# Delta heads through tanh inside local attention's steps, and the first projection block loaded in halves

## The reference

```python
def ab_mixer(u, w_in, conv_w, a_log, dt_bias, a_out_g, bq_g, bk_g, sink, w_out):
    proj = u @ w_in
    qa, ka, va, za, ba, aa, qb, kb, vb = split_cols(proj, AB_SIZES)
    ya = delta_mixer(qa, ka, va, za, ba, aa, conv_w, a_log, dt_bias, a_out_g)
    ...
    yb = window_mixer(qb, kb, vb, sink)
    return jnp.concatenate([ya, yb.astype(ya.dtype)], axis=-1) @ w_out

def delta_mixer(hq, hk, hv, hz, hb, ha, conv_w, a_log, dt_bias, o_gain):
    qkv = jax.nn.silu(centred_conv(jnp.concatenate([hq, hk, hv], axis=-1), conv_w))
    q, k, v = split_cols(qkv, (A_QKW, A_QKW, A_VW))
    q = l2norm(q.reshape(bsz, n, A_HEADS, A_DK)) * (A_DK ** -0.5)
    k = l2norm(k.reshape(bsz, n, A_HEADS, A_DK))
    ...
```

## Time and profile before

| | us |
|---|---|
| three runs | 1564.33, 1565.94, 1567.14; median 1565.94 |
| the profiled execution | 1562.62 |
| its span | 1560.8 |
| busy: PE, PEld | 1520.3 (97%), 1471.7 (94%) |
| busy: DVE, ACT, POOL | 1099.1 (70%), 798.1 (51%), 173.7 (11%) |
| local attention's steps and the tail behind them | 54 to 142 |
| the delta stage | 142 to about 245 |

### The profile page before, as it was taken

How to read it: one execution, slowest core, us unless ns; L and a number is a source line. 1 busy time by engine, 2 the same in 40 slices (tenths; PEclk the granted TensorE clock), 3 DMA queues, 4 the chain that set the end, 5 groups by cost and what they waited for, 6 DMA issues and landing times.

```text
span 1560.8 us, 31984 instructions
## 1 busy us (share of the span) xinstructions
PE 1520.3 (97%) x12908; PEld 1471.7 (94%) x12908; DVE 1099.1 (70%) x1965; ACT 798.1 (51%) x1369; POOL 173.7 (11%) x187
## 2 busy tenths in 40 slices
PE   6988999999999999999999999999999999999997
PEld 5977899999998999999998999999999999999997
DVE  5784758676778677778778667776668666666666
ACT  4766445343455544446545655444555556554443
POOL 2481203000021200002000201000010010200000
PEclk9998999999999999999999999999999999999999
DMA  6420016454441345454433424656444444356561
GB/s 223 163 109 1 3 55 213 174 184 180 162 162 68 109 169 208 162 202 176 163 137 134 166 101 141 216 165 209 168 162 163 162 164 161 109 176 202 166 210 58
DMA packets 124791, 236.35 MB, mean 151 GB/s; under 512 B 2614, under 2 KB 50025, under 8 KB 124665
## 3 DMA queue, kind: packets, MB, share of 16 engines
q1 hardware_dynamic: 123177, 230.24, 42.2%
q0 software_dynamic: 1296, 4.28, 0.9%
q10 hardware_dynamic: 192, 0.05, 0.0%
HBM read 233.51 MB, written 1.05 MB: 150 GB/s over the span
## 4 chain that ended last, share of the span: by engine, by line
PE 88%; DVE 6%; ACT 2%; issue 2%; POOL 1%; DMA 0%; ACTq 0%; DVEq 0%; POOLq 0%
PE ps L675 49%; PE ps L722 6%; PE ps L721 6%; PE ps L720 6%; PE ps L683 6%; PE ps L844 2%; DVE w_lo L2511 2%; PE ps L821 1%; PE ps L771 1%; PE ps L806 1%; DVE hidden L2562 1%; PE ps L831 1%; POOL square_sum L3567 0%; DVE chain_memory L3124 0%; ACT w_hi L1771 0%
## 5 line engine op out<-in xcount | busy, mean ns | idle before, releaser
L1771 ACT ACTIVATE w_hi<-raw 128x1024 fp32r<-128x1024 f32 x440 | 460.6, 1051 | 282.1 <-PE ps L722 135.3
L2511 DVE TENSOR_TENSOR w_lo<-raw,w_hi 128x1024 fp32r<-128x1024 f32 x440 | 547.0, 1243 | 9.4 <-ACT w_hi L1771 9.1
L675 PE MATMUL ps<-u_hi,w_hi 128*128 128x256 f32 (+1 forms) x1464 | 422.6, 289 | 1.9 <-issue 1.2
L675 PE MATMUL ps<-u_hi,w_lo 128*128 128x256 f32 (+1 forms) x1464 | 416.8, 285 | 0.0
L675 PE MATMUL ps<-u_lo,w_hi 128*128 128x256 f32 (+1 forms) x1464 | 416.3, 284 | 0.0
L675 PEld LDWEIGHTS ps<-u_hi,w_hi 128*128 128x128 f32 x1464 | 278.0, 190 | 8.0 <-issue 5.6
L675 PEld LDWEIGHTS ps<-u_hi,w_lo 128*128 128x128 f32 x1464 | 278.1, 190 | 0.0
L675 PEld LDWEIGHTS ps<-u_lo,w_hi 128*128 128x128 f32 x1464 | 277.0, 189 | 0.6
L675 PE MATMUL ps<-a_hi,w_hi 128*128 128x256 f32 x800 | 226.7, 283 | 0.6 <-DVE hidden L2562 0.3
L675 PE MATMUL ps<-a_lo,w_hi 128*128 128x256 f32 x800 | 224.9, 281 | 0.0
L675 PE MATMUL ps<-a_hi,w_lo 128*128 128x256 f32 x800 | 224.8, 281 | 0.0
(11 more groups left out here) (469 smaller groups left out, 2257.1 us busy)
## 6 DMA issues: line engine op xcount, KB each, us to landing
raw<-in_w_ff_dram SPq DMA_DIRECT2D x32, 2048.0 KB, 7.7
raw<-in_ffn_w_gu_dram SPq DMA_DIRECT2D x44, 1024.0 KB, 6.9
raw<-in_ffn_w_down_dram SPq DMA_DIRECT2D x10, 2048.0 KB, 8.0
raw<-in_xa_w_kv_dram SPq DMA_DIRECT2D x8, 2048.0 KB, 8.3
raw<-in_od_w_in_dram SPq DMA_DIRECT2D x6, 2048.0 KB, 7.8
raw<-in_w_in_ab_dram SPq DMA_DIRECT2D x5, 2048.0 KB, 7.9
raw<-in_ev_w_in_dram SPq DMA_DIRECT2D x5, 2048.0 KB, 7.8
raw<-in_xa_w_q_dram SPq DMA_DIRECT2D x4, 2048.0 KB, 7.6
```

The costliest lines, as they stand in the source:

```text
L675: mm = pe.matmul(bank[:, 0:n], wx[:, q, k * P:(k + 1) * P], x[ux][:, k, ts], start=k == 0 and i == 0, stop=k == KD - 1 and i == 2)
L1771: act.activation(quarter(w_hi, b, q), raw_quarter(b, q), ACT.Copy).then_inc(high_split, 1)
L2511: dve.tensor_tensor(quarter(w_lo, b, q), raw_quarter(b, q), quarter(w_hi, b, q).bitcast(F32), ALU.subtract)\
```

## The change

1. The SiLU over all heads becomes x (1 + tanh(x / 2)), twice the SiLU, in three parts of four heads. ScalarE makes the tanh (`half_tanh`) and VectorE the product (`double_silu`): queries in step 3, keys with the tanh in step 5 and the product in step 6, values with the tanh at the end of step 6 and the product in step 8. The factor two is taken out in the squares, in `delta_norm` and in the values' copies. A table set that has both tanh and exponential is loaded in step 2; the set with the logarithm behind the values' tanh.
2. The squares go to steps 4 (queries) and 6 (keys); both are waited for before the key sum.
3. Chunk 11 is convolved as the others are, its products on ScalarE in step 6, its additions on GpSimd.
4. From step 5 on the order changes on three engines: the scores of units 7 and 8 and the key sum come earlier on TensorE; the exponentials of units 7 and 8 come directly behind the copies of pair 6 on ScalarE; on VectorE pair 7's logits come ahead of two tile reads.
5. GpSimd's identity tiles wait for the query sum too.
6. Block 2 is loaded as two halves of 256 columns. The first is issued when two quarters of block 0 are split, and ScalarE waits for it alone before the first two quarters.

```diff
@@ weights, SyncE and ScalarE
-    add("ab_qkvz", [[cols(x, c)] for c in range(0, 2048, BLOCK)])
+    add("ab_qkvz", [[cols(x, 0, 256), cols(x, 256, 256, into=256)]] + [[cols(x, c)] for c in range(BLOCK, 2048, BLOCK)])
...
+                if b == phases["ab_qkvz"].first:
+                    for half, (into, width, source) in enumerate(loads):
+                        sp.wait_ge(low_split, 4 * (b - 2) + 2 * half + 2)
+                        sp.dma_start(raw[:, b % 2, :, into:into + width], source)\
+                            .then_inc(raw_in[b % 2] if half else first_half_in, 16)
+                    return
@@ TensorE
-                pe.wait_ge(M["d_sq"], which + 1)
+                pe.wait_ge(M["d_sq"], 2)
...
+                    pe.wait_ge(M["silu_done"], SILU_TURN[VALUE_HEADS])
@@ ScalarE
+            def half_tanh(which):
+                act.wait_ge(M["conv_done"], 4 * SILU_TURN[which])
+                act.activation(delta_tanh[which], delta_heads[which], ACT.Tanh, scale=0.5).then_inc(M["delta_tanh"], 1)
+            def head_squares(which):
+                act.wait_ge(M["silu_done"], SILU_TURN[which])
+                act.activation(delta_sq[which], delta_heads[which], ACT.Square, scale=0.5).then_inc(M["d_sq"], 1)
...
-                    act.wait_ge(M["conv_done"], 8 if c == 10 else c - 3)
+                    act.wait_ge(M["conv_done"], {10: 8, 11: 10}.get(c, c - 3))
...
+                if k == 5:
+                    half_tanh(KEYS)
+                if k == 6:
+                    conv_products(11)
                 if k < WINDOW_UNITS:
                     window_copies(k)
                 if k == 6:
-                    act.wait_ge(M["conv_done"], 11)
-                    act.wait_ge(M["conv_last"], 1)
-                    act.activation(qkv, qkv, ACT.Silu).then_inc(M["silu_done"], 1)
+                    window_exponents(7)
+                    head_squares(KEYS)
+                    window_exponents(8)
+                    half_tanh(VALUE_HEADS)
                     log_and_exp()
@@ VectorE
+            def double_silu(which):
+                dve.wait_ge(M["delta_tanh"], SILU_TURN[which])
+                dve.scalar_tensor_tensor(delta_heads[which], delta_tanh[which], 1.0, delta_heads[which], ALU.add, ALU.mult)\
+                    .then_inc(M["silu_done"], 1)
...
-                if k == 5:
-                    last_conv()
@@ GpSimd
-            for c in range(11):
+            for c in range(12):
...
-            pool.wait_ge(M["conv_done"], 11)
+            pool.wait_ge(M["conv_done"], 12)
+            pool.wait_ge(M["d_qsum"], 2)
```

More of the change, by code:

```diff
@@ L395, in program @@
             for i, loads in enumerate(ph.blocks):
-                so_far[len(landed_at) % 2] += 16 * len(loads)
+                halved = len(landed_at) == phases["ab_qkvz"].first
+                so_far[len(landed_at) % 2] += 16 if halved else 16 * len(loads)
                 landed_at.append(so_far[len(landed_at) % 2])
@@ L1464, in _ @@
             for k in range(WINDOW_UNITS + 1):
-                if k < WINDOW_UNITS and k != 7:
+                if k < 7:
                     window_scores(k)
-                if k < 7:
                     qkvz_tile(2 * k + 2)
+                if k == 6:
+                    window_scores(7)
                 if k == 0:
@@ L1484, in _ @@
                 if k == 6:
[L1485 removed]
+                    window_scores(8)
                     qkvz_tile(15)
+                if k == 7:
+                    delta_sum(KEYS)
                 if k == 8:
@@ L1766, in split_high @@
                     return
-                if q == 0:
+                halved = b == phases["ab_qkvz"].first
+                if halved and q == 0:
+                    act.wait_ge(first_half_in, 16)
+                if q == (2 if halved else 0):
                     act.wait_ge(raw_in[b % 2], looped(landed_at[b], LOOP_LANDED, g))
@@ L2128, in _ @@
                     next_split(1)
-                if k < 6:
+                if k < 5:
                     conv_products(2 * k)
-                if k < WINDOW_UNITS:
+                if k < 7:
                     window_exponents(k)
+                if k == 5:
+                    conv_products(10)
+                if k == 2:
+                    nc.scalar.preload_act_table_set("exp_and_others")
+                if k == 3:
+                    half_tanh(QUERIES)
+                if k == 4:
+                    head_squares(QUERIES)
                 if k < 6:
@@ L2146, in _ @@
                     conv_products(2 * k + 1)
-                if k == 7:
-                    act.wait_ge(M["silu_done"], 1)
-                    for which in (KEYS, QUERIES):
-                        act.activation(delta_sq[which], delta_heads[which], ACT.Square).then_inc(M["d_sq"], 1)
+                if k == 5:
+                    half_tanh(KEYS)
+                if k == 6:
+                    conv_products(11)
                 if k < WINDOW_UNITS:
@@ L2163, in _ @@
                 act.activation((v_tok if source == 8 else k_tok)[0:n, m], tile_bank[i % 4][0:n, 0:4 * P].rearrange(
-                    "p (h d) -> p h d", h=4), ACT.Copy).then_inc(M["d_copied"], 1)
+                    "p (h d) -> p h d", h=4), ACT.Copy, scale=0.5 if source == 8 else 1.0).then_inc(M["d_copied"], 1)
             def decays(chain):
@@ L2846, in _ @@
             ab = phases["ab_qkvz"].first
-            def last_conv():
-                link(dve.tensor_scalar(qkv[:, 11], xa[:, 11, 0:T], col("conv", 11), None, ALU.mult))
-                for j in range(1, 5):
-                    ins = dve.scalar_tensor_tensor(qkv[:, 11], xa[:, 11, j:j + T], col("conv", 12 * j + 11), qkv[:, 11],
-                                                   ALU.mult, ALU.add)
-                    if j < 4:
-                        link(ins)
-                ins.then_inc(M["conv_last"], 1)
             def project_qb(i, t, gt):
@@ L2962, in delta_norm @@
                 dve.wait_ge(M["d_rs"], which + 1)
-                dve.scalar_tensor_tensor(heads, heads, P ** -0.5 if which == QUERIES else 1.0,
+                dve.scalar_tensor_tensor(heads, heads, 0.5 * P ** -0.5 if which == QUERIES else 0.5,
                                          delta_r[which].rearrange("p h t -> p (h t)"), ALU.mult, ALU.mult)\
                     .then_inc(M["d_normed"], 1)
+            def double_silu(which):
+                dve.wait_ge(M["delta_tanh"], SILU_TURN[which])
+                dve.scalar_tensor_tensor(delta_heads[which], delta_tanh[which], 1.0, delta_heads[which], ALU.add, ALU.mult)\
+                    .then_inc(M["silu_done"], 1)
             dve.wait_ge(M["sink_meta"], 1)
             for k in range(WINDOW_UNITS + 1):
-                if k < WINDOW_UNITS:
+                if k < 7:
                     window_logits(k)
-                if k < 8:
+                if k < 6:
                     qkvz_step(2 * k + 1)
+                if k == 6:
+                    double_silu(KEYS)
+                if k == 7:
+                    window_logits(8)
                 if k < WINDOW_UNITS:
                     window_normalise(k)
+                if k == 6:
+                    window_logits(7)
+                    qkvz_step(13)
+                if k == 7:
+                    qkvz_step(15)
+                if k == 8:
+                    double_silu(VALUE_HEADS)
                 if k == 1:
```

22 lines of the change are left out of this document (12 added, 10 removed).

## The result

The changed kernel takes 1555.83 us (median of 5 runs, 1555.29 to 1560.35), the kernel before, run beside it, 1566.09 (5 runs, 1564.33 to 1567.14). The ratio is 0.9947, with a 95% interval of 0.9936 to 0.9959: 10.3 us faster. The forecast was 1557.5, in a range of 1552.5 to 1562. In a second session five more runs of the changed kernel had a median of 1556.57, against 1564.43 for before (0.9951, 0.9939 to 0.9964).

A forecast was written before the change was run, and what follows sets the result against it. TensorE was taken as the bound, except in the local-attention tail, where waits on VectorE and ScalarE leave holes. The delta stage 8.4 us earlier takes the median from 1565.94 to 1557.5; 8-in-10 range 1552.5 to 1562.

The forecast's parts named there:

- Pairs 2 to 5 cost nothing: Local attention up to pair 5: added ScalarE and VectorE work fits in 8.65 us pairs, TensorE stays the bound; no change.
- Pair 6: Pair 6's transposes start at 110.4, not 115.28: 4.9 us won, nearly all from the convolution removed from VectorE.
- The queue that carries the tail: GpSimd's additions end at 119.0, then values' tanh to 120.1, table load to 121.4, copies 7 to 122.3, key logarithms to 123.9.
- The sums: Key and query sums on TensorE: 2.1 us each at full clock, plus half a microsecond for one at low clock.
- Together: The whole tail: delta stage starts at 134.0 instead of 142.43, 8.4 us earlier.
- The load in halves, 0 with a possible guard of up to 3.3: Block 2's load near 40 us: only ScalarE's idle time goes, counted 0; slack 0.3 us, at most 3.3 against later landings.
- The rest of the span as long as before (1418.4): Sign of being right: everything from the delta stage's start to the end keeps its length, 1418.4 us.
- The slower rival, GpSimd late: Tail additions averaging 1.55 us make GpSimd 12.7 late: 4.3 slower, 1570.2; chance 0.04.
- The convolution's going: Removing VectorE's 3.7 us convolution beside GpSimd was to pay back up to 2.6 us lost to two double SiLUs.

The follow-up runs named there:

- conv_off: The kernel before with chunk 11's convolution moved from VectorE to ScalarE and GpSimd, SiLU and block 2's load still whole; 1565.06 us, ratio 1.0005.
- halves_only: The kernel before with block 2 loaded in halves and nothing else; 1564.78 us, ratio 1.0006.
- before_again: The kernel before, unchanged, run again for a second profile; 1565.13 us, ratio 0.9996.
- pool_longer: The changed kernel with three of chunk 11's products made by GpSimd instead of ScalarE; 1559.33 us, ratio 0.9967 to before.
- whole_load: The changed kernel with block 2 loaded whole again, everything else kept; 1562.70 us, ratio 0.9985 to before.
- whole_again: The changed kernel with block 2 loaded whole, a second time; 1561.65 us, ratio 0.9971 to before.
- whole_late_small: The changed kernel with block 2 loaded whole and GpSimd's four small loads issued only after it has landed; 1562.22 us, ratio 0.9977 to before.
- combined: The changed kernel, halves kept, GpSimd's small loads behind block 2's landing, result 6 and copies 7 ahead of the values' tanh; 1559.54 us, ratio 0.9963 to before.
- early_copies: The changed kernel with pair 6's result and pair 7's copies on ScalarE ahead of the values' tanh and table load; 1556.33 us, ratio 0.9953 to before.
- spin: The changed kernel with five unused 272-column matmuls on TensorE behind the key sum; 1557.90 us, ratio 0.9954 to before.

## Why the prediction was right, point by point

- *Pairs 2 to 5 cost nothing:* right. VectorE was put at 8.5 and measured 8.58, ScalarE at 7.8 and 7.71, TensorE busy throughout. Pair 6's scores start 70.6 us behind the head sum in both kernels.
- *Pair 6:* transposes predicted at 110.4, found at 110.89; pair 7's at 118.7 and 118.01; the key sum at 119.4 and 118.61. The working gave nearly all of pair 6's gain to the removed convolution. At pair 6 that holds (3.4 us by conv_off), but not at the end: conv_off's time is that of before.
- *The queue that carries the tail:* the right queue, and a little short. Convolution 9 was to end at 110.6, and ended at 112.1. The additions took 1.02 each, less than the 1.06 assumed, but their unbroken run now begins at 106.06 and not at 104.20. The addition beside the queries' double SiLU is 0.9 longer than the median, which accounts for half of that delay, and the one beside the keys' adds 1.1 within the run. So the values' tanh started 1.35 after the predicted end of GpSimd at 119.0, and the logarithms at 123.58 instead of 122.3. That the table load costs 1.28 and no drain held: the tanh ends at 121.46, the load at 122.75, and the next activation starts at 122.77. The Trainium skill ("ScalarE: Activation LUTs", What ACT_TABLE_LOAD costs) would add 1.38 there; this trace does not agree.
- *The sums:* half a microsecond was put in for a low clock. In this execution the query sum alone took 3.83 for 2.1, as the window at 0.50 shows. To offset it, the turned tiles ran at full clock, 2.79 instead of 4.46: from the first turn to the delta stage 3.7, where 5.2, measured at a granted clock of 0.66, was assumed. And a term was missing: pair 7's values and unit 8's transposes (2.4 us from 123.72) stand on TensorE between pair 7's copies and the query sum, which began at 126.10, 0.95 behind the end of the logarithms.
- *Together:* the delta stage 8.4 earlier was predicted. It was 6.6 in the first profile (135.84 against 142.43) and 8.1 in the second (134.35). In the first profile the errors are 1.3 (logarithms), 0.95 (the missing term) and 1.2 (clock) the one way and 1.5 (turned tiles) the other, 1.8 in all. That they cancel in part is luck.
- *The load in halves, 0 with a possible guard of up to 3.3:* the step that was mis-sized. Against the kernel before it is 0 (halves_only), but only as that kernel's block is in time. Loaded whole in the changed kernel the block lands 3 us later, and without the halves 5 to 7 us of the 10 would have been lost: 2.5 to 2.7 of wait and 1.7 of low clock on the path, the rest not located. The time was met only because the change carried the halves. The working saw the 0.3 us of slack and named the halves a guard. It did not ask what would make the block later in the new kernel, and its chances had no rival for it.
- *"The rest of the span as long as before (1418.4)":* wrong as a check. 1418.4 was a lucky rest: before_again had 1422.0, the changed kernel 1422.7 and 1420.7. The difference of medians was 10.3 in the first session and 7.9 in the second, that of leads 6.7 and 8.0. In the first the changed kernel's profile was of its slowest run, so the two need not agree. The forecast, made from the median of before, stayed right.
- *The slower rival, GpSimd late:* did not happen, and its place was the right one: at 1.02 per addition ScalarE waits 2.89 us there, and pool_longer shows that a further delay goes straight into ScalarE's wait. In the working's own sum GpSimd sets the tail even without being late; the 8.4 us of this rival are what would use up the whole gain. The Trainium skill ("SBUF — State Buffer", Who interferes with whom) has a VectorE instruction with two inputs in SBUF and a GpSimd instruction that reads SBUF take turns, which the prediction took as up to 2.6 us for the two double SiLUs. The trace agrees in kind: the additions beside them took 1.70 and 1.85 instead of 0.78, 2.0 us in all. In the 14 profiles every addition or product of a convolution on GpSimd that took over 1 us, 198 of them, lay beside a double SiLU or a split (`split_low`, 1.2 to 1.7 us, two inputs in SBUF as well). The mean of 1.02 against 1.06 hides this, as both runs have such neighbours. The convolution's going did not pay it back, as the working had it: the four additions beside it before took 0.90 each, 0.5 us too much in all.

```profile
106.71 3.61 POOL L3595 TENSOR_TENSOR mx<-mx 128x272 f32<-128x272 f32 x4
```

No run moves the double SiLUs away from GpSimd's additions, so what the tail would gain by it is not measured.

## What to carry to other kernels

When an engine's queue has one long operation over data of several producers, splitting it so that only the last part stands behind the last producer is worth more than moving the producer: here the split and its order gave nearly all the gain, the moved convolution 1 to 2 us by the medians, within their intervals. When a queue of small instructions on GpSimd bounds a stage, look at its longest ones and at what VectorE does beside them; a mean over the queue hides them. Where a transfer is in time by a few tenths of a microsecond, guard it in the same change, since another edit may delay it, as happened here, and count a hole in TensorE with the low clock behind it. Before comparing parts of two profiles, look at the granted clock of the parts that were not changed: two profiles of one kernel differed by 3.6 us there.

## What the runs showed of the hardware

- A hole of 2.0 to 2.7 us in TensorE in a stretch that was otherwise busy was followed by a granted clock of 0.66 to 0.93 in the next windows, which cost another 1.7 us (whole_load, whole_again, whole_late_small, combined). Not every such hole is: in early_copies the query sum behind one of 2.51 us ran at full clock (2.10).
- GpSimd's additions over 128x272 took 0.78 us in the median. All 198 additions and products of the convolutions that took over 1 us in the 14 profiles (1.5 to 1.9) lay beside a VectorE instruction that reads two operands of 1024 or 1088 columns in SBUF.
- Full clock in the tail and a short rest did not go together: halves_only and spin had it there, and rests of 1423.4 and 1421.8; before and conv_off had 0.66 in the tail's last 5 us, and rests of 1418.4 and 1418.8. But before_again had 0.68 there and 1422.0 all the same. What decides where the low clock falls was not settled.
- A 64 KB load in 64-byte pieces took 4.4 to 9.5 us. Between 30 and 34 us, with it under way beside block 2, the core's DMA moved 3 and then 200 GB/s in windows that were 0.75 and 0.88 busy (whole_again), and 365 in the next; in before_again it was 73 and 260, at 0.86 and 0.75.
